# A hybrid decoder step: sample queries with the rows held in TensorE, and the second expert layer's first gathers issued in the first layer

## The reference, cut to what matters

```python
def peer_ffn(xn, w_q, sub_keys, u_tab, v_tab):
    q = (x2 @ w_q).reshape(T, PEER_HEADS, 2, PEER_HALF)
    s = jnp.einsum('thpd,hpnd->thpn', q, sub_keys)
    sv, si = lax.top_k(s, PEER_TOPK)
    ...
    top_s, top_i = lax.top_k(cand, PEER_TOPK)
    idx = jnp.take_along_axis(cidx, top_i, axis=-1).reshape(T, PEER_HEADS * PEER_TOPK)
    gate = jax.nn.softmax(top_s, axis=-1).reshape(T, PEER_HEADS * PEER_TOPK)
    def block(args):
        h = jnp.einsum('td,ted->te', xb, u_tab[ib])
        act = jax.nn.gelu(h, approximate=False) * gb
        return jnp.einsum('te,ted->td', act, v_tab[ib])
```

## Time and profile before

| | |
|---|---|
| median of 3 runs | 3906.41 us (3898.76 to 3907.11) |
| the profiled execution's own time | 3903.53 us |
| its span | 3901.7 us |
| TensorE busy, granted clock | 67%, 0.771 |
| VectorE, ScalarE, GpSimd busy | 62%, 41%, 35% |
| moved by DMA | 1276.43 MB, 327 GB/s over the span |
| first expert layer's loop ends, second's begins | about 2118 us, 2277 us |

### The profile page before, as it was taken

One profiled execution on the slowest core, in us unless ns is written; L12 is line 12 of the kernel. 1 busy time (PEld: TensorE's weight loads), 2 busy tenths in 40 slices (PEclk: granted clock), 3 DMA queues, 4 the chain that ended last, 5 costly groups with the idle time before them and its releaser, 6 DMA issues. The chain is left out here.

```text
span 3901.7 us, 52707 instructions
## 1 busy us (share of the span) xinstructions
PE 2631.5 (67%) x17989; PEld 1436.6 (37%) x17989; DVE 2436.1 (62%) x6110; ACT 1593.1 (41%) x4447; POOL 1346.7 (35%) x1188
## 2 busy tenths in 40 slices
PE   7998788764554566667665656566657767666666
PEld 6876776321111122223222322223213334334343
DVE  2565542677766767767767237677766666666653
ACT  2362111443333344445533134355435545544431
POOL 0003430344444434333433024333443344443331
PEclk9998878886565677777787777678778878877756
DMA  2211002899999999999998379999999999999995
GB/s 92 70 58 56 13 13 71 325 411 419 417 415 415 408 388 418 413 400 395 405 407 362 113 290 402 370 403 405 414 405 418 384 413 414 419 417 404 409 413 220
DMA packets 241815, 1276.43 MB, mean 327 GB/s; under 512 B 32904, under 2 KB 75152, under 8 KB 105872
## 3 DMA queue, kind: packets, MB, share of 16 engines
q0 software_dynamic: 154880, 1133.58, 71.1%
q1 hardware_dynamic: 86672, 139.52, 10.1%
HBM read 1258.51 MB, written 14.36 MB: 326 GB/s over the span
## 5 line engine op out<-in xcount | busy, mean ns | idle before, releaser
L1907 POOL DMA_INDIRECT ring<-in_uv,idx x1024 | 1153.1, 1126 | 1970.1 <-PE acc L2398 1558.9
L2157 DVE SCALAR_TENSOR_TENSOR ring<-ring,rep 128x1024 f32<-128x1024 f32 x1024 | 1236.1, 1221 | 521.9 <-DMA ring<-in_uv,idx 438.2
L2398 PE MATMUL acc<-ring,diag 128*32 128x512 f32 x4096 | 752.8, 818 | 992.6 <-ACT diag L2006 991.7
L1998 ACT ACTIVATE hg<-hs 128x1 f32<-128x1 f32 x1024 | 204.6, 200 | 1242.6 <-DVE ring L2157 1240.0
L2398 PEld LDWEIGHTS acc<-ring,diag 128*32 128x32 f32 x4096 | 91.8, 122 | 1282.0 <-ACT diag L2006 1235.8
L2006 ACT ACTIVATE diag<-const,hgg 128x32 f32<-128x32 f32 x1024 | 329.3, 322 | 33.4
L2285 PE MATMUL big<-xnT,w 128*128 128x256 f32 (+1 forms) x992 | 322.7, 463 | 4.0 <-ACT rep L1948 3.1
L2002 ACT ACTIVATE hgg<-hg,weigh_by 128x1 f32<-128x1 f32 x1024 | 302.0, 295 | 33.4
L2285 PEld LDWEIGHTS big<-xnT,w 128*128 128x128 f32 x992 | 205.1, 225 | 157.8 <-issue 129.5
L300 PE MATMUL acc<-xnT,w 128*128 128x260 f32 x1024 | 230.8, 386 | 0.7 <-ACT inp L421 0.7
L300 PEld LDWEIGHTS acc<-xnT,w 128*128 128x128 f32 x1024 | 196.5, 192 | 38.4 <-issue 7.4
(11 more groups left out here) (581 smaller groups left out, 4252.5 us busy)
## 6 DMA issues: line engine op xcount, KB each, us to landing
w<-in_w_peer SPq DMA_DIRECT2D x80, 512.0 KB
w<-in_w_gdn SPq DMA_DIRECT2D x32, 512.0 KB, 3.3
ring<-in_uv,idx POOLq DMA_INDIRECT x1024, 12.7
wo<-in_w_mla_out SPq DMA_DIRECT2D x12, 1024.0 KB, 19.3
wo<-in_w_uq SPq DMA_DIRECT2D x8, 768.0 KB, 21.6
sk<-in_keys SPq DMA_DIRECT2D x80, 64.0 KB
out_ssm_s<-states SPq DMA_DIRECT2D x4, 1024.0 KB, 5.1
wo<-in_w_gdn_out SPq DMA_DIRECT2D x4, 1024.0 KB, 6.9
```

The source lines that it names most:

```text
L1907: pool.indirect_dma_start(out=ring[:, c % RING, :], out_offset=None, in_=uv, in_offset=bass.IndirectOffsetOnAxis(ap=idx[u % 2][:, c:c + 1] ...
L1998: act.activation(hg[a][:, c:c + 1], hs[a][:, c:c + 1], ACT.Gelu).then_inc(s["gelu"], 1)
L2157: dve.scalar_tensor_tensor(ring[:, c % RING, 0:D], ring[:, c % RING, 0:D], 1.0, rep[:, 4 * a + 2 * (c // RING) + c % 2, :], ALU.mult, ALU. ...
L2398: last = pe.matmul(acc[i][subs(j, b), :], diag[:, r - 1 + b, :], ring[:, r - 1 + b, D + HALF * j:D + HALF * j + HALF], start=r == 1, stop= ...
```

## The change

The diff does four things.

1. The sample sweep of layer 1. The sample rows are the held operand (8 columns) and the weights of both halves of a head move, 256 columns in one matmul; the result is 8 rows, copied to `sq_row` by ScalarE, turned by two small transposes, copied again, and scored as before. A head takes two slots where it took four (`ask_at(h) = ASK + 2 h`). The weights of heads 0 and 5 use `w`, those of the others free parts of `wo`, the keys of all heads come at once into `oT`; the loads of heads 1 to 4 are issued together after the output projection of the samples.
2. With the sweep ended at slot 498, the four stages of the samples' top-16 move into the loop, at slots 503, 506, 509 and 511, and the first two repeated sample rows as well.
3. Layer 0 lays and places unit `UNITS` itself, between its sample rows, and GpSimd issues the first 8 gathers of layer 1 at the end of layer 0, when the samples' sum has freed the ring. Ring, indices, gates and the two small tables are carried from layer to layer, with a semaphore per ring buffer (`ahead`). Layer 1 begins without `lay`, `place` and its first 8 gathers.
4. `load_up` of the second half stands at the start of layer 1, ahead of the first weights, and the norm's gain behind them. To make room, `mla_layer` puts `wk` into `oT` and allocates `q`, `wukT` and the norm's rows for shorter times.

```diff
     def sync(self, sp, m):
                 sp.dma_start(self.kr[:, :, :], kept["kr"]).then_inc(s["held"], 16)
-                self.load_up(sp)
...
+TOP_LAST = TOPK * (UNITS - 1) + 7
...
-def ask_at(h, p):
-    return ASK + 4 * h + 2 * p + 2 * min(h, 1)
+def ask_at(h):
+    return ASK + 2 * h
...
 class Carried:
+        self.counting = core.sbuf(ctx, "counting", [P, TOPK])
+        self.same = core.sbuf(ctx, "same", [P, NS, NS])
+        self.idx = [core.sbuf(ctx, "idx", [P, TOPK], U32) for _ in range(2)]
+        self.weigh_by = [core.sbuf(ctx, "weigh_by", [P, TOPK]) for _ in range(2)]
+        self.ring = core.sbuf(ctx, "ring", [P, RING, 2 * D])
+        self.ahead = Marks(core, "ahead", **{f"r{c}": 16 for c in range(RING)})
...
+        def sample_weights(h):
+            if h in (0, 5):
+                return w[:, :, :, :]
+            i = 2 * ((h - 1) % 5) if h < 5 else 2 * (h - 6)
+            return wo[:, i:i + 2, :].rearrange("p a (k n) -> p a k n", k=KD)
...
                 if opens:
                     load_out(wd)
-                load_gain(layer)
+                    load_gain(0)
+                else:
+                    back.load_up(sp)
...
+                def load_query(h):
+                    for p in range(2):
+                        sp.dma_start(sample_weights(h)[:, p, :, :], weight[2 * h + p]).then_inc(s[f"sw{h}"], 16)
...
                 for p in range(2):
                     load(first, p)
-                sp.dma_start(counting[:, :], core.i["counting"]).then_inc(s["inp"], 16)
-                sp.dma_start(same[:, :, :], core.i["same"]).then_inc(s["inp"], 16)
+                if opens:
+                    sp.dma_start(counting[:, :], core.i["counting"]).then_inc(s["inp"], 16)
+                    sp.dma_start(same[:, :, :], core.i["same"]).then_inc(s["inp"], 16)
+                else:
+                    load_gain(1)
...
+                        if n == ASK - 14:
+                            after(sp, at("q_made", HEADS - 2, 2), paged.at("v_turned", HALVES, 0))
+                            load_query(0)
+                            sp.dma_start(oT[:, 4:8, :], keys.rearrange("p (h a) n -> p h (a n)", a=4)).then_inc(s["sk_in"], 16)
+                        if n == OWN + 9:
+                            after(sp, (s["o_made"], GROUPS - base))
+                            for h in range(1, 5):
+                                load_query(h)
                         for h in range(H):
-                            for p in range(2):
-                                if n == (ask_at(h - 1, p) + 1 if h else ASK - 14 + 4 * p):
-                                    after(sp, at("sq_made", h - 1, p + 1) if h else at("q_made", HEADS - 2, p + 1), at("scored", UNITS - 3 + 2 * min(h, 1) - first, 1))
-                                    load(HEADS + h, p)
-                            if n == ask_at(h, 1) + 4:
+                            if n == ask_at(h) + 1 and h < 3:
+                                after(sp, at("sq_made", h, 1))
+                                load_query(h + 5)
+                            if n == ask_at(h) + 6:
                                 gather_scores(h)
...
             def _(pool):
+                        if not opens and u == 0 and c < RING:
+                            continue
...
+                if opens:
+                    after(pool, at("placed", UNITS, 1), (s["spv"], 1))
+                    for c in range(RING):
+                        pool.indirect_dma_start(out=ring[:, c, :], out_offset=None, in_=core.i["uv1"],
+                                                in_offset=bass.IndirectOffsetOnAxis(ap=idx[0][:, c:c + 1], axis=0)).then_inc(ahead[f"r{c}"], 16)
...
             def _(act):
+                    if n == ask_at(h) + 1:
+                        after(act, at("sq_made", h, 1), at("sq_turned", h - 1, 0))
+                        act.activation(sq_row(h), pq[:NS, 0:2 * P], ACT.Copy).then_inc(s["sq_row"], 1)
+                    if n == ask_at(h) + 3:
+                        after(act, at("sq_turned", h, 1), at("sscored", h - 1, 0))
+                        act.activation(sqT[:, h % 2, :, :], spare[:, 0:2 * NS].rearrange("p (a b) -> p a b", a=2), ACT.Copy).then_inc(s["sq_out"], 1)
+                    if n == ask_at(h) + 5:
                         copy_scores(h, sample_scores(h))
...
+                            if n == TOP_LAST + 5:
+                                weigh_samples()
...
             def _(dve):
+                        if not opens and u == 0 and c < RING:
+                            dve.wait_ge(ahead[f"r{c}"], 16)
...
+                            sample_top({0: 0, 3: 1, 6: 2, 8: 3}.get(n - TOP_LAST))
...
-                if late_sample:
-                    for stage in range(4):
-                        sample_top(stage)
                 for b in range(NS):
...
+                    if b == 4 and opens:
+                        place(UNITS)
...
             def _(pe):
+                    if n == ask_at(h):
+                        pe.wait_ge(s[f"sw{h}"], 32)
+                        after(pe, at("sq_row", h - 1, 1))
+                        for kk in range(KD):
+                            last = pe.matmul(pq[:NS, 0:2 * P], xnT[:, kk, HALF_ROWS:], sample_weights(h)[:, :, kk, :], start=kk == 0, stop=kk == KD - 1)
+                        last.then_inc(s["sq_made"], 1)
+                    if n == ask_at(h) + 2:
+                        after(pe, at("sq_row", h, 1), at("sq_out", h - 1, 1))
                         for p in range(2):
-                            last = pe.matmul(sample_scores(h)[:, p, :], sqT[:, h % 2, p, :], sk[:, h % 2, p, :], start=True, stop=True)
+                            last = pe.transpose(spare[:, NS * p:NS * p + NS], sq_row(h)[:, P * p:P * p + P], core.const[:NS, C_ID, 0:NS])
+                        last.then_inc(s["sq_turned"], 1)
...
                 else:
-                    lay(0, 0, index)
-                    lay(0, 1, gate)
                     for i in range(8):
                         repeat(0, i)
...
+                            if n == TOP_LAST + 7:
+                                flip_samples()
+                            if u == UNITS - 1 and c in (13, 14):
+                                sample_row(c - 13)
...
                 for b in range(2, NS):
+                    if b == 4 and opens:
+                        after(pe, at("top", UNITS, TOP_STEPS))
+                        lay(UNITS, 0, index)
+                    if b == 6 and opens:
+                        after(pe, at("gate", UNITS, 2))
+                        lay(UNITS, 1, gate)
...
 def program(nc, ins, outs):
-        peer(core, 0, oT, os, core.i["w_gdn_out"], kept, carried)
-        mla_layer(core, kept)
-        peer(core, 1, oT, os, core.i["w_mla_out"], kept, carried)
+        with carried.ahead:
+            peer(core, 0, oT, os, core.i["w_gdn_out"], kept, carried)
+            mla_layer(core, kept, oT)
+            peer(core, 1, oT, os, core.i["w_mla_out"], kept, carried)
```

More of the change, by code:

```diff
@@ L1720, in peer @@
         rep = core.sbuf(ctx, "rep", [P, 8, D])
-        ring = core.sbuf(ctx, "ring", [P, RING, 2 * D])
+        ring, ahead = carried.ring, carried.ahead
         k = TopK(core, ctx, P)
-        idx = [core.sbuf(ctx, "idx", [P, TOPK], U32) for _ in range(2)]
-        weigh_by = [core.sbuf(ctx, "weigh_by", [P, TOPK]) for _ in range(2)]
+        idx, weigh_by = carried.idx, carried.weigh_by
         hs = [core.sbuf(ctx, "hs", [P, TOPK]) for _ in range(2)]
@@ L1891, in _ @@
                             load_gain(1)
-                for h in range(H):
-                    if late_sample and ask_at(h, 1) + 4 >= UNITS * TOPK:
-                        gather_scores(h)
                 for e in range(2):
@@ L1900, in _ @@
                 for u in range(UNITS):
-                    after(pool, at("placed", u, 1))
+                    after(pool, at("placed", u - first, 1))
                     for c in range(TOPK):
@@ L1970, in place_gates @@
                 def place_gates(v):
-                    after(act, at("mixed", v, 2))
+                    after(act, at("mixed", v - first, 2))
                     if v >= 2:
@@ L2153, in _ @@
                             after(dve, at("rep_out", tile_of(u), 8))
[L2154 removed]
+                        if not opens and u == 0 and c < RING:
+                            dve.wait_ge(ahead[f"r{c}"], 16)
+                        after(dve, at(f"landed{c % RING}", u, 16 * (c // RING + 1 - first)))
                         if u >= 2:
@@ L2303, in score @@
                     hh, t = v // 2, v % 2
-                    after(pe, (s["first_out"], 2 * t + 2 if opens else 0) if hh == 0 else at("q_out", hh - 1, 2), at("top", v - first, 0), at("gated", v, 0))
+                    after(pe, (s["first_out"], 2 * t + 2 if opens else 0) if hh == 0 else at("q_out", hh - 1, 2), at("top", v - first, 0), at("gated", v - first, 0))
                     if hh > H and not late_sample:
@@ L2313, in lay @@
```

(11 more changed lines are left out.)

79 lines of the change are left out of this document (28 added, 51 removed).

## The result

The changed kernel takes 3877.49 us, median of 6 runs (3872.42 to 3882.63), beside 3906.12 us for the kernel before (6 runs, 3890.62 to 3910.57): a ratio of 0.9929, 95% interval 0.9916 to 0.9942. A second set on another occasion gave 3881.12 us and 0.9940 (0.9926 to 0.9954). So it is faster by 0.5 to 0.8%, and the forecast of 3876 us was met. Its parts were not: the layer change cost 16 us more than forecast, the tail gained 5 us less, and the loop together with three smaller differences made up for both.

What follows compares the result with a forecast made beforehand. DMA transfers were taken to bound both expert layers' loops, so time is won only where their share falls. The terms summed to -30.2 us: 3903.5 to 3873.3, or 3876 us with the median's 2.9; range 3862 to 3894.

Steps and rivals of the forecast that it cites:

- First layer's tail: End of the first layer: two `lay` groups between sample rows and a `place` between dot products cost +1.0 us.
- Eight gathers from the first layer's end: Layer's last barrier waits for GpSimd, whose eight issues end about 9.2 us behind the samples' addition: +9.2 us (8.8 to 10).
- a layer change 10 to 16 us longer: Sign of being right: the stretch between the samples' addition and the norm's end grows by 10 to 16 us.
- The norm's gain: Attention front end: the gain's load lands later beside the moved gathers, +3 us (0 to +6).
- Second layer's start: First dot product waits only for the repeated rows, ready at 2263.2 in place of 2277.49: -14.3 us (-11 to -15).
- `w_uk` and `w_uv`: Loads moved to the second layer's start, onto empty DMAs; TensorE's wait shortens: -11.2 us (-5 to -13).
- Sweep and last slots: Second layer's late loop: sample sweep in two slots per head, top-16 between dot products 503 and 511: +2.5 us (-3 to +10).
- The first rival: Slots 478 to 494: TensorE at 1.2 GHz bounds the sweep, a pair of slots takes 11.5 us; 3918 us, chance 0.07.
- The third rival: Second layer: TensorE stands as long for a kept latent as for `w_uv`, only bytes are saved; 3882 us, chance 0.08.
- The tail: End of the second layer: sample gathers start 0.5 us behind dot product 511, not 21.45: -20.9 us (-18 to -21).
- the first sample gather within 2 us of the last dot product: Sign of being right, at the end of the second layer's loop.
- The second rival: Samples' top-16 stays on the path, VectorE's dot products queue behind it, tail wins 9 to 11 us less; 3886 us, chance 0.13.

Runs made afterwards that it cites:

- e9: Changed kernel with the eight early gathers issued at the start of the last block before the second expert layer, which makes the decode queries; 3859.3 us.
- e1: Changed kernel with the second layer's first eight gathers issued at its own start again, all else kept; 3864.6 us.
- e7: Changed kernel with both the eight gathers and the loads of `w_uk` and `w_uv` back where they were before; 3874.2 us.
- e5: The changed kernel itself, unaltered, run again on another chip; 3881.1 us, ratio to the kernel before 0.9926 to 0.9954.
- e4: Changed kernel with the second layer's two first sample rows moved behind the last slot; 3880.1 us.
- e3: Changed kernel with the eight gathers moved from the first layer's end into the block that makes the latents, behind the landing of `w_uq`; 3856.1 us.

## Why the prediction was right, and where it was wrong

*First layer's tail: right.* The two pairs of sample dots that hold a `lay` start 2.28 us apart, the others 1.72: +1.1 for +1.0.

*Eight gathers from the first layer's end: wrong, by 15.7 us.* The step that failed is "the layer's last barrier waits for GpSimd", read as waiting for its issues. The barrier opens only when the gathers have landed: 27.67 us with eight, 17.43 with four, 2.75 with none, and again in another block (e9). The forecast's own sign, a layer change 10 to 16 us longer, failed with it: it is 25 us longer. Which part of the block's end does the waiting, GpSimd's own end or the clearing of the semaphores, is open.

*The norm's gain: 0.4 in place of +3, for another reason.* It landed at once (1.09 us of waiting, as before), since the gathers were through when it was issued. So the Trainium skill's rule of turns between queues (page "DMA: Bandwidth & Descriptors", section "Queues, rings and completion order") was not put to the test here.

*Second layer's start: right in size (-13.5 for -14.3), and its reason half right.* The tables and the placed index do it; the full ring that the prediction put beside them isn't needed (e1, e7: 10.8 and 10.7 us without it). "From there the ring is as full as it was before, so what follows has the same order" was wrong: a ring full at the first dot left the DMAs idle until a slot came free (share 0.46 over 16 us).

*`w_uk` and `w_uv`: right.* The wait went from 15.80 to 4.4 us, -11.4; undoing it cost 15.2 us, and 5 to 10 without the early gathers.

*Sweep and last slots: right as a sum.* From dot 464 to 511 it is 141.1 us before and 142.8 after (143.6 in e5), +1.7 to +2.5 for +2.5. Inside it two things cancel that I had not told apart: up to dot 503 the changed kernel loses 8 us, and from there to 511 it takes 21.4 us in place of 27.5. The DMAs are full through both sweeps (1.02 in the earlier trace rows and above); what differs is when the weights come. From dot 464 to 503 SyncE's queue moves 5.94 MB before and 9.50 MB after (DMA view of the two stretches: packets, MB, share):

```profile
q1 hardware_dynamic: 2941, 5.94, 13.6%
```

```profile
q1 hardware_dynamic: 2576, 9.50, 19.5%
```

The 3.56 MB between them are 8.6 us at 414 GB/s, the 8 us lost; the kernel before moves most of them between dots 503 and 511. So the streamed weights don't make the loop shorter; they end the sweep early enough for the top-16 to stand in the loop, and the gain appears in the tail. No run takes the sweep alone back, so that this needs the new sweep is argued from the traces and not shown.

The first rival (TensorE bound at 1.2 GHz) didn't come: the granted clock was 0.93, and pairs of slots from 478 to 494 took 5.0 to 8.2 us, 5.9 on average. By the Trainium skill (page "TensorE: Matmul & The Clock Gate", section "HAM oscillation — how this bites in real kernels") bursts of matmuls parted by waits for DMA fall back to the lower clock. The trace agrees at one place only: behind a wait of 3.89 us eight sums took 1.93 us, at a granted clock of 0.50, in place of 1.06. But TensorE was busy 46.62 of the 53 us, so the sweep as a whole was not such a case, and the rival's reading of it was wrong.

```profile
3751.93 1.93 PE L2438 MATMUL acc<-ring,diag 128*32 128x512 f32 x8 [3.89 <-ACT diag L2046]
```

The third rival (a kept latent in place of `w_uv`) came with 4.4 us and not with 15.8.

*The tail: wrong by 5 us.* "The last index is made after dot product 511, so sample gathers start 0.5 us behind it" left out what the index waits for on TensorE: a sample row of 3.60 us that the listing issues one slot before the turn. The sign "the first sample gather within 2 us of the last dot product" failed with 5.55. Moving the rows gave 3.1 of it back; the remaining 2 us are the turn itself (1.02 us at a granted clock of 0.50 in e4) and its place behind the last dot. The second rival had the right consequence, a smaller tail gain, by way of VectorE; it was TensorE.

*Why the sum was right all the same.* By luck in part. The 15.7 and 5.0 us that were lost against the forecast were set off by 12.6 more gain than forecast in the loop (7 by the second profile), 4.8 in the stretch up to the first layer's end, whose length differs by several us between executions that share its code (the addition ends between 2138.0 and 2149.9 among these runs), 2.6 in the attention front end and 1.5 behind the first sample gather. The loop's 12.6 is only in part explained: by the table of distances 3.4 of it lie between dots 0 and 32, where the wait for `w_uv` went, 4.3 between 32 and 96, where executions differ, and 4.9 between 96 and 464, where the forecast had no term; the first dot's term and the sweep's missed by 0.8 each in opposite directions. A total that agrees is no evidence for its terms. The forecast had named the check: "a long gap ahead of the attention projections, which would say that the early gathers cost what they win". That gap is there, and they cost more.

## What to carry to other kernels

Where stages are closed by a barrier as here, gathers that GpSimd issues in one stage for the next are waited for at that barrier; a load that SyncE issued was not (e3). Put them into a block that lasts longer than they do and leaves the DMAs idle, as in e3, which won 21 to 25 us with the same eight gathers. And in a loop bound by transfers, price a prefetch by the idle DMA time that it removes less the idle time that it makes, not by when the first consumer starts.

## What was not expected of the hardware

The end of a block took in the landing of the gathers that GpSimd issued in it: 18.0 us of standstill behind the last of eight issues, in which no engine has an instruction and the DMAs move about 400 GB/s for the first 13. Two executions of the same code differ most at one place of the loop, between dots 64 and 96 (101.8 us in the first profile of the change, 106.9 in that of e4); the DMA share there is 0.99 and 0.93, so the longer one holds idle DMA time, and what decides that was not tried.
